# A layer kernel's first block: four more landing places for weight pieces, modulation work moved, the last output pieces and the norm done by 128 tokens

## What is computed

```python
mod = silu(c) @ w_ada + b_ada
sh_m, sc_m, gt_m, sh_f, sc_f, gt_f = split(mod, 6)
h = rms_norm(x, g_pre_mix) * (1 + sc_m) + sh_m
proj = h @ w_in                                # q, k, v of the two attentions "a" and "b"
mix = concat(fox_attention(...), moba_attention(...))
x = x + gt_m * rms_norm(mix @ w_out, g_post_mix)
h = rms_norm(x, g_pre_ffn) * (1 + sc_f) + sh_f
top_v, top_i = top_k(h @ w_router + b_router, 4)
y = sum over the 4 experts of gate * (swiglu(h @ w_gate_up[e] + b) @ w_down[e] + b)
x = x + gt_f * rms_norm(y, g_post_ffn)
# then two further blocks, which the change leaves as they are
```

## Time and profile before

| | |
|---|---|
| median of 3 runs | 2080.53 us (2080.02 to 2083.95) |
| the profiled execution, its own time | 2079.61 us |
| its span | 2077.8 us |
| busy: PE, DVE, ACT, POOL | 94%, 43%, 35%, 28% |
| first block up to the expert loop | 0 to 234 us |
| expert loop, 35 turns | 234 to about 1205 us |
| two further blocks | the rest |

### The profile page before, as it was taken

One profiled execution on the slowest core, in us unless ns is written; L12 is line 12 of the kernel. 1 busy time (PEld: TensorE's weight loads), 2 busy tenths in 40 slices (PEclk: granted clock), 3 DMA queues, 4 the chain that ended last, 5 costly groups with the idle time before them and its releaser, 6 DMA issues.

```text
span 2077.8 us, 28169 instructions
## 1 busy us (share of the span) xinstructions
PE 1951.1 (94%) x10657; PEld 1197.2 (58%) x10658; DVE 893.8 (43%) x1383; ACT 721.7 (35%) x1181; POOL 586.1 (28%) x622
## 2 busy tenths in 40 slices
PE   5997799999999999999998889999999999999998
PEld 2974333333333333333332259889888798898887
DVE  4644322111122222112211157557787566576983
ACT  2543211111111111111111055664665456556662
POOL 3230234433433434424434404000133021000440
PEclk7998799999999999999999989999999999999999
DMA  9978699999898999999999975446456553544553
GB/s 343 302 281 346 252 397 417 418 418 417 343 417 330 419 417 418 394 377 418 418 417 417 419 234 198 124 159 203 143 182 208 173 194 121 184 160 145 191 195 121
DMA packets 203045, 609.34 MB, mean 293 GB/s; under 512 B 10459, under 2 KB 115055, under 8 KB 166385
## 3 DMA queue, kind: packets, MB, share of 16 engines
q1 hardware_dynamic: 197360, 585.14, 73.8%
q0 software_dynamic: 5280, 22.19, 3.0%
q10 hardware_dynamic: 328, 0.95, 0.1%
HBM read 607.17 MB, written 9.26 MB: 297 GB/s over the span
## 4 chain that ended last, share of the span: by engine, by line
PE 71%; DMA 11%; SPq 6%; DVE 6%; ACT 4%; issue 2%; POOL 1%; ACTq 0%; DVEq 0%
PE bank L860 21%; PE bank L1192 15%; PE bank L897 10%; PE bank L1216 9%; DMA side<-in_w_gate_up 8%; PE bank L899 5%; SPq L699 4%; PE bank L1143 3%; SPq L706 2%; PE bank L1156 1%; DMA ring<-in_w_down 1%; DVE split L1662 1%; PE bank L1184 1%; PE bank L967 1%; ACT split L2101 1%
## 5 line engine op out<-in xcount | busy, mean ns | idle before, releaser
L1192 PE MATMUL bank<-ring,qkv 128*64 128x512 f32 x2240 | 504.2, 598 | 32.6 <-POOL ring L2384 32.5
L1192 PEld LDWEIGHTS bank<-ring,qkv 128*64 128x64 f32 x2240 | 152.5, 137 | 366.4 <-issue 268.8
L1662 DVE TENSOR_TENSOR split<-ring,split 128x2048 fp32r<-128x2048 f32 x104 | 249.9, 2403 | 115.5 <-ACT split L2101 115.5
L897 PE MATMUL bank<-hT_both,split 128*128 128x512 f32 x800 | 285.9, 401 | 6.7 <-DVE split L1662 6.7
L1216 PE MATMUL bank<-ring,qkv 128*64 128x512 f32 x1120 | 248.5, 595 | 1.3 <-DMA ring<-in_w_down 1.1
L2101 ACT ACTIVATE split<-ring 128x2048 fp32r<-128x2048 f32 x104 | 199.2, 1916 | 131.1 <-PE bank L860 126.1
L899 PE MATMUL bank<-hT_both,split 128*128 128x256 f32 x800 | 225.8, 282 | 0.0
L1636 DVE TENSOR_SCALAR qkv<-bank 128x512 f32<-128x512 f32 x35 | 24.2, 692 | 446.3 <-PE bank L1192 446.3
L2073 ACT ACTIVATE qkv<-qkv 128x512 f32<-128x512 f32 x35 | 22.1, 631 | 531.2 <-DVE qkv L1636 531.2
L1650 DVE SCALAR_TENSOR_TENSOR out_halves<-bank,small,out_halves 64x512 fp32r<-64x512 f32 x70 | 52.5, 750 | 330.2 <-ACT out_halves L2084 329.7
L897 PEld LDWEIGHTS bank<-hT_both,split 128*128 128x128 f32 x800 | 151.6, 190 | 45.1 <-DVE split L1662 8.0
(11 more groups left out here) (358 smaller groups left out, 3046.9 us busy)
## 6 DMA issues: line engine op xcount, KB each, us to landing
ring<-in_w_down SPq DMA_DIRECT2D x150, 1024.0 KB, 17.2
ring<-in_w_gate_up SPq DMA_DIRECT2D x70, 1024.0 KB, 19.8
probs<-in_w_gate_up SPq DMA_DIRECT2D x62, 1024.0 KB, 17.8
ring<-in_w_in SPq DMA_DIRECT2D x58, 1024.0 KB, 5.4
ring<-in_w_up SPq DMA_DIRECT2D x44, 1024.0 KB, 5.1
consts<-in_w_gate_up SPq DMA_DIRECT2D x31, 1024.0 KB, 20.5
side<-in_w_gate_up SPq DMA_DIRECT2D x31, 1024.0 KB, 22.4
qkv<-in_w_gate_up SPq DMA_DIRECT2D x31, 1024.0 KB, 21.7
```

Source lines behind the costliest of these rows:

```text
L897: pe.matmul(b[:, :].rearrange("p (h t) -> p h t", h=2), w_high[:, k, rows], hT_both[:, :, k, :], start=(k == 0), stop=False, skip_group_ch ...
L1192: last = pe.matmul(hidden[q][CAP * j:CAP * j + CAP, :], xgT[:, k % 4, k // 4, :], unit_at(k)[:, c:c + 512], start=False, stop=(k == KC - 1 ...
L1662: dve.tensor_tensor(low, unit_at(u % RING_L), high.bitcast(F32), ALU.subtract).then_inc(low_done, 1)
```

## The change

- Units get a home by table (`first_slots`). Units 26 to 29 go to places outside the ring: the `bands` constants, `qkv[:, 0:2048]`, `side`, `htok`. 25 to 29 can all be issued once the `w_in` product is through (27 after the scores of "a", 29 after the transposes of h). Units 30 to 33, 38, 39 take slots 2, 3, 4, 5, 0, 1; 34 to 37 take 2, 3 and the homes of 26 and 28. Each waits for the unit before it in its own slot.
- The last two `w_out` units become 38 and 39 in PE's count and 34 to 37 are the second half of modulation 2, but SP issues 38 and 39 ahead of 34.
- PE does modulation 1 and the first half of modulation 2 together, then `ada_rows(1)`, then the values of "b". Modulation 2's bank is held over that time.
- The last two `w_out` units are multiplied first for tile 0 only; then come the second half of modulation 2, unit 38 for tile 1, `ada_rows(2)`, unit 39 for tile 1.
- Norm, modulation and transposes go by tile. The modulated h is now x * gain, then * rstd + shift, so that the first pass needs no root. `turn_h` gives way to `turn_tile`; ACT copies g0 to g2, DVE g3.
- Expert units go out as slots come free: 4 and 5 of expert 0 after the second `w_out` unit, 2 and 3 two units later, staged 3 and 5 two after that; then 0, 1 and 8 to 11 after all 40; 6 and 7 after h and mod11.

```diff
+def first_slots():
+    at_bands, at_qkv, at_side, at_htok = range(RING, RING + 4)
+    order = [*range(FIRST_OUT_1 + 2), *OUT_1[2:], *range(FIRST_OUT_1 + 2, LAST_OUT_1)]
+    slots = {u: u % RING for u in range(26)}
+    slots.update({26: at_bands, 27: at_qkv, 28: at_side, 29: at_htok, 30: 2, 31: 3, 32: 4, 33: 5, 38: 0, 39: 1,
+                  34: 2, 35: 3, 36: at_bands, 37: at_side})
...
-            for u, source in enumerate(sources):
+            for u in first_order:
...
-                if u >= RING:
-                    sp.wait_ge(unit_done, u - RING + 1)
+                if first_held[u] is not None:
+                    sp.wait_ge(unit_done, first_held[u] + 1)
+                elif u == 26:
+                    sp.wait_ge(unit_done, KC + len(IN1))
+                elif u == 27:
+                    sp.wait_ge(*full("ascore17"))
+                elif u == 29:
+                    sp.wait_ge(*full("h3"))
...
             sp.wait_ge(*full("bturn7"))
-            for u in (0, 1, 3, 5):
+            for u in (0, 1):
                 load_staged(1, u)
             sp.wait_ge(*full("bout3"))
             load_staged(1, 4)
+            sp.wait_ge(unit_done, 33 + 1)
+            for u in (4, 5):
+                load_unit(0, u)
+            sp.wait_ge(unit_done, 35 + 1)
+            for u in (2, 3):
+                load_unit(0, u)
+            sp.wait_ge(unit_done, 37 + 1)
+            for u in (3, 5):
+                load_staged(1, u)
             sp.wait_ge(unit_done, first.units)
-            for u in range(RING):
+            for u in (0, 1, 8, 9, 10, 11):
                 load_unit(0, u)
             sp.wait_ge(h_ready, 3)
             sp.wait_ge(*emptied("mod11"))
-            for u in range(RING, MOE_UNITS):
+            for u in (6, 7):
                 load_unit(0, u)
...
-            ada(1)
+            ada_units(1, range(KC))
+            ada_units(2, range(KC // 2))
+            ada_rows(1)
             values("b", lambda h, c: proj1["vb"][:, c, h * DH:h * DH + DH])
-            ada_units(2, range(KC // 2))
...
+            for u in range(2):
+                mixed_in(u)
+                used(out_product(u, next_halves(2), range(4)))
+            last_halves = {}
+            for u in range(2, 4):
+                mixed_in(u)
+                last_halves[u] = unit_halves(2, OUT_1[u])
+                last = out_product(u, last_halves[u], (0, 1))
+            last.then_inc(tile_rows, 1)
             ada_units(2, range(KC // 2, KC))
+            used(out_product(2, last_halves[2], (2, 3)))
             ada_rows(2)
+            used(out_product(3, last_halves[3], (2, 3)))
             for tt in range(TT):
-                pe.wait_ge(h_ready, seen(h_ready))
-            turn_h([f"g{j}" for j in range(4)], htok)
+                turn_tile("g", tt)
...
-            post_norm([f"mix{j}" for j in range(4)], gate_m, x_mid)
+            def tile_modulated(tt):
+                dve.wait_ge(x_mid, seen(x_mid))
+                dve.tensor_tensor(htok[:, tt, :], x[:, tt, :], gain_f, ALU.mult)
+                tile_rstd(tt)
+                dve.scalar_tensor_tensor(out=htok[:, tt, :], in0=htok[:, tt, :], scalar=rstd[:, tt:tt + 1], in1=shift_f,
+                                         op0=ALU.mult, op1=ALU.add).then_inc(h_ready, 1)
+            layer_rows("mix", 0, gate_m)
+            layer_scaled("mix", 0, x_mid)
             ada(2, 2 * [gain(gain_f, gpre_f)])
             await_own("mod9")
-            await_x_mid()
-            row_scale()
-            modulated(gain_f, shift_f)
+            tile_modulated(0)
+            layer_rows("mix", 1, gate_m)
+            layer_scaled("mix", 1, x_mid)
+            tile_modulated(1)
+            await_full("g3")
+            leave(dve.tensor_copy(hT[:, 4:8, P:2 * P], bank("g3")[:, :].rearrange("p (k t) -> p k t", k=4)), "g3")
             ada_rows(2, 2, 2 * [gate(gate_f, gpost_f)])
...
-            square_banks([bank(f"mix{j}")[:, :] for j in range(4)], lambda: await_full("mix3"))
-            square_x(x_mid_ready)
-            for j in range(4):
-                copy(f"g{j}", hT[:, 2 * j:2 * j + 2, :])
+            act.activation(spare, eps, ACT.Sqrt)
+            layer_squares("mix", 0)
+            post_root(0)
+            pre_root(0, x_mid)
+            layer_squares("mix", 1)
+            post_root(1)
+            for g in range(2):
+                copy(f"g{g}", hT[:, 4 * g:4 * g + 4, 0:P])
+            pre_root(1, x_mid)
+            copy("g2", hT[:, 0:4, P:2 * P])
```

More of the change, by code:

```diff
@@ L147, in halves_slots @@
     return slots, owner
+def first_slots():
[4 more added lines that the diff above has]
+                  34: 2, 35: 3, 36: at_bands, 37: at_side})
+    turns, held_by, holds = {}, {}, {}
+    for u in order:
+        of_slot = holds.setdefault(slots[u], [])
+        held_by[u] = of_slot[-1] if of_slot else None
+        of_slot.append(u)
+        turns[u] = len(of_slot)
+    return order, slots, turns, held_by
 class Plan:
     def __init__(self):
-        self.tiles, self.units, self.jobs, self.uses, self.at = 0, 0, {}, [0] * 8, 0
+        self.tiles, self.units, self.jobs, self.uses, self.at, self.held = 0, 0, {}, [0] * 8, 0, None
     def bank(self, name):
+        if self.at % 8 == self.held:
+            self.at += 1
         b = self.at % 8
@@ L213, in ada_units @@
     def ada_units(r, n):
-        p.bank(f"ada{r}")
+        if f"ada{r}" not in p.jobs:
+            p.bank(f"ada{r}")
         for k in range(n):
@@ L240, in plan_first, with two_modulations @@
     p.attention("a", lambda: project(IN1[6:]))
[L241 to L242 removed]
+    def two_modulations():
+        ada_units(1, KC)
+        ada_units(2, KC // 2)
+        p.held = p.jobs["ada2"][0]
+        ada_rows(1)
+    p.attention("b", two_modulations)
     for j in range(4):
         p.bank(f"mix{j}")
[L245 removed]
+    for u in range(2):
         p.unit(*[f"mix{j}" for j in range(4)])
[L247 to L248 removed]
+    ada_units(2, KC // 2)
+    p.held = None
     ada_rows(2)
+    for u in range(2):
+        p.unit(*[f"mix{j}" for j in range(4)])
     for j in range(4):
@@ L1356, in row_scale @@
                 own(dve.reciprocal(rstd, root))
-            def post_norm(names, gate, signal):
-                mean_squares(names, gate, lambda last, j: leave(last, names[j]), bank)
-                row_scale()
-                await_own(names[-1])
-                for tt in range(TT):
-                    scaled(tt).then_inc(signal, 1)
-            def mean_squares(names, gate, done, bank_of):
-                for j, n in enumerate(names):
-                    tt, half = j // 2, slice(512 * (j % 2), 512 * (j % 2) + 512)
-                    dve.wait_ge(squares, seen(squares))
-                    if j == 3:
-                        pair = halves.rearrange("p (t a) -> p t a", t=TT)
-                        dve.tensor_tensor(meansq, pair[:, :, 0], pair[:, :, 1], ALU.add).then_inc(means, 1)
-                    done(dve.tensor_tensor(htok[:, tt, half], bank_of(n)[:, :], gate[:, half], ALU.mult), j)
             def scaled(tt, half=slice(0, D)):
@@ L1379, in scaled, with weighted, tile_rstd, layer_rows @@
                                                 in1=x[:, tt, half], op0=ALU.mult, op1=ALU.add)
-            def await_x_mid():
-                seen(x_mid)
-                dve.wait_ge(x_mid, seen(x_mid))
+            def weighted(tt, sources, gate, done):
+                for half in range(2):
+                    columns_ = slice(512 * half, 512 * half + 512)
+                    dve.wait_ge(squares, seen(squares))
+                    if half == 1:
+                        dve.tensor_tensor(meansq[:, tt:tt + 1], halves[:, 2 * tt:2 * tt + 1],
+                                          halves[:, 2 * tt + 1:2 * tt + 2], ALU.add).then_inc(means, 1)
+                    done(dve.tensor_tensor(htok[:, tt, columns_], sources[half], gate[:, columns_], ALU.mult), half)
+            def tile_rstd(tt):
+                dve.wait_ge(roots, seen(roots))
+                own(dve.reciprocal(rstd[:, tt:tt + 1], root[:, tt:tt + 1]))
+            def layer_rows(prefix, tt, gate):
+                if tt == 0:
+                    dve.wait_ge(tile_rows, seen(tile_rows))
+                else:
+                    await_full(f"{prefix}3")
+                names = [f"{prefix}{2 * tt + half}" for half in range(2)]
+                weighted(tt, [bank(n)[:, :] for n in names], gate, lambda last, half: leave(last, names[half]))
+            def layer_scaled(prefix, tt, signal):
+                tile_rstd(tt)
+                await_own(f"{prefix}{2 * tt + 1}")
+                scaled(tt).then_inc(signal, 1)
             dve.memset(eps, EPS)
@@ L1677, in hT_low @@
                     leave(last, n)
-            def weighted(tt, sources, gate, done):
-                for half in range(2):
-                    columns_ = slice(512 * half, 512 * half + 512)
-                    dve.wait_ge(squares, seen(squares))
-                    if half == 1:
```

(6 more changed lines are left out.)

134 lines of the change are left out of this document (56 added, 78 removed).

## The result

| | before | changed |
|---|---|---|
| median of 7 runs of each | 2080.02 us (2075.92 to 2083.95) | 2067.59 us (2065.86 to 2074.68) |
| the profiled execution | 2079.61 us | 2066.44 us |
| its span | 2077.8 us | 2064.6 us |

The ratio is 0.995, with a 95% interval of 0.9938 to 0.9963: the change takes 10.4 us off by the ratio, and 7.7 to 12.9 by the interval; the two medians are 12.4 us apart. The forecast was 2070.8 us, with a gain of 9.3. Of all runs on record one was slow, an execution of e4_loads_late (3535.55 us at a granted clock of 0.562); it is left out of that kernel's median and ratio.

What follows compares the result with a forecast made beforehand. Late `w_out` loads after DMA holes, then the norm tail, delay the expert loop, whose start moves everything. Router's result 9.3 us earlier, routing unchanged: 2079.61 - 9.3 = 2070.3, plus half the median's 0.9 offset: 2070.8; range 2067.5 to 2074.

Steps and rivals of the forecast that it cites:

- rival D: PE's clock stays up in the shorter gaps (2.5 us) and rises sooner in the first turn (1): 2067.3; chance 0.05.
- Loads up to the product: From 129.1 five units go out at once instead of one; product starts at 165.6, 5.1 us earlier.
- The product: 96 output matmuls 24.3 us, four modulation units 3.5, `ada_rows(2)` 1.1: end at 194.5, only 0.5 earlier.
- The tail: Norm, modulation and transposes after the product: last pass ends 201.2 for 209.34, router's result 205.2 for 214.46, 9.3 earlier.
- The tightest place: DVE modulates tile 0 to 195.1, just before tile 1's first square is there at 195.3; slack 0.2 us.
- The gate between g3 and the router's result: DVE's gate from mod10 and mod11, 1.28 us, formerly covered by transposes, now delays the router's result from 204.5 to 205.2.
- Routing: Router's result to first turn's bias: same instructions, unchanged at 19.9 us, so the bias starts at 225.1 for 234.34.
- The first turn: First turn of the expert loop: the moment PE's clock rises there can fall out 1.5 us either way.
- The cover: Expert loads land by 221.2, PE needs unit 0 at 227.1; if cover were gone, each microsecond late costs one.
- A: Order of work gains nothing up front, product still starts about 170.7; only norm by tile pays, 4.4: 2075.7; chance 0.11.
- B: Loads bind the loop's start, and PE's gain comes back as waits before L1192: about 2080; chance 0.07.
- C: Slower: PE reaches the expert loop at half clock, rising late; about 2090 if held through first turn; chance 0.04.

Runs made afterwards that it cites:

- e4_loads_late: Changed kernel, with all twelve ring loads of expert 0 and staged 3 and 5 issued only after all 40 units and h are ready; 2070.48 us, ratio 0.9947.
- e5: Kernel before, with POOL's subtraction for the low half of the experts' bias held back until PE has filled `places`; 2075.95 us, ratio 0.9984.
- e2: Changed kernel's tile order of product and norm, but old six slots, old modulation order and late expert loads; 2073.33 us, ratio 0.9974.
- e11: Changed kernel plus 8 needless matmuls ahead of the output product, to keep PE's clock up; 2067.78 us, ratio 0.9958.
- e10: Changed kernel, with all eighteen expert loads ahead of the loop issued as one block after the routing's `turned_gates`; 2085.57 us, ratio 1.0041.
- e1: The changed kernel once more, no edit; 2068.53 us, ratio 0.9955.
- e3: Kernel before plus the homes, moved modulation and expert loads as slots come free; product and norm as before; 2071.88 us, ratio 0.9969.

## Why the prediction was right

The mechanism and nearly every step held; the number was helped by luck. 2067.59 lies 3.2 us below the forecast, 0.1 inside the low end of the forecast's own range (2067.5 to 2074), and nearer to rival D's 2067.3, whose reason did not come about. And the start of the first turn, 225.1 forecast and 224.66 measured, is that near because two errors cancel: the router's result came 1.1 us late and the routing was 1.5 us shorter. Predicted and measured, in the changed kernel (whose trace is 0.46 us late already at the end of the `w_in` product, before anything that the change touches):

| step | predicted | measured |
|---|---|---|
| values of "b" start | 154.0 | 154.6 |
| product starts | 165.6 | 166.01 |
| product and what is in it end | 194.5 | 195.7 |
| last pass of the modulation ends | 201.2 | 202.43 |
| router's result taken | 205.2 | 206.28 |
| first turn's bias | 225.1 | 224.66 |
| whole time | 2070.8 | 2067.59 |

- **Loads up to the product.** Right: twelve units without a wait on DMA, and the product released by DVE's low copy.
- **The product.** 1.2 us late, 0.46 of it inherited. Its slow start stayed, as assumed; 72 matmuls took 19.17, where the prediction's terms give 18.9 (24.3 less 5.4), and each twelve of tile 1 took 2.95 for 2.7. `ada_rows(2)` did not wait: DVE's copy of the modulation row ended at 189.5, PE came at 191.70, slack 2.2 for a predicted 2.0.
- **The tail.** The tightest place was named with a slack of 0.2, and there was none: DVE's second pass over tile 0 ended at 196.49, and ACT had ended tile 1's first square at 196.35. It cost some 0.1 to 0.3. The 0.2 was a slip in the sum: from PE at `ada_rows(2)` (190.7) its own terms, 1.1 for the rows, 1.4 for the gains and two passes of 1.24, give 195.7 and not 195.1, which is after the square at 195.3. The gate between g3 and the router's result cost as said in kind, but only 0.2 of the 0.7 I had put there, since PE's router product ended at about 206.1 anyhow.
- **Routing.** "The same instructions", 19.9 us: this was the wrong step. The instructions were the same and took 18.4, for they stood otherwise to POOL's list. The prediction moved DVE's and PE's work past each other and did not lay POOL's three instructions beside it; e5 shows the cause, and it was worth 1.0 us in the changed kernel; the other 0.5 is clock.
- **The first turn.** Sized at no change, with 1.5 us either way. It was 2.8 us shorter, with the clock up before its first matmul. Over 14 profiles it is 28.53 to 28.55 in nine, all with the clock up before it. In four the clock rose only within the turn: 3.0 us into it in e2 (29.90), 5.8 in e4 (31.30), 6.0 in the kernel before (31.37) and 6.4 in e11 (31.58), so each microsecond at half clock cost a little under a half. The fourteenth, e10's 29.92, had the clock up and is longer by its two waits for loads. Neither the kernel nor the start decides when the clock rises: e4 and e1 differ by 2.8 us with the same program on PE. The band for this place was too narrow.
- **The cover.** Right in its result and too strict in its reason. I let it end where a unit is needed; e4 and e10 show that the reserve is the queue's idle time, about 21 us, and that what goes beyond it is paid in turns 2 to 6, which become DMA-bound, and not at the first turn's waits.
- **Rivals.** A (nothing won up front) is what e2 has, and its 0.9974 is 5.4 us for the 4.4 worked out; the changed kernel isn't there. B (the expert stream takes the gain) fell: the three more waits of the profiled run are absent in e1, and across all kernels but e10 the count wanders from 61 to 66 whatever the start. C (slower by the clock) fell; where the clock was at its worst, in e11, the first turn was 3.0 us longer than the changed kernel's, with the clock back at 229.4, 6.4 us into it. D was half there: the clock did not stay up at the product, but rose before the first turn.

The 10.4 us of the ratio agree with the 9.7 of the earlier start: 8.2 of them by the steps of the prediction, which had 9.3 there, and 1.5 in the routing, where it had none. What the profiled run has beyond that, the first turn's 2.8 and the 2.9 us behind the loop, is spread that other profiles show in either direction (the rest is 896.0 to 900.7 us in code that no experiment touches). How much of the difference the first turn's clock makes stays open: one profile per kernel can't say how often each length occurs. The mean granted clock of whole executions gives an estimate: it was 0.9789 over the 68 executions of the kernel before that were run beside the experiments and 0.9804 over 11 of the changed one (e1 included), and among the 68 a thousandth more of clock went with 1.3 us less of time. By that some 2 us of the difference go with the clock, in whatever stretch.

## What to carry to other kernels

Here a prefetch was worth as much as the loader's idle time ahead, not as the time until the consumer asks for the first piece. So count the idle time, and in a loop that turns between a bound by the engine and a bound by loads count the waits, each of which costs the difference of the two paces. When a step is moved, lay the lists of all engines beside it, POOL's too, since a vector instruction that starts beside a POOL one may have to sit that one out, in a stretch that nobody touched. Work put in to hold a clock has to end before the engine would be released anyway; else it eats what the clock gives.

## What the hardware showed that I had not expected

- DVE beside a POOL instruction: 0.42 to 1.46 us (two SBUF inputs), 0.17 to 0.58 in e5 and to 1.06 in e3 (a cast of 16 columns), 0.20 to 1.02 (tensor_scalar on 64 columns); an instruction with one of its inputs in a bank stayed at 0.20. In each case the DVE instruction ended 0.03 to 0.28 us after the POOL one, so a DVE instruction of 0.2 us can lose 0.8 or 0.9.
- An fp32 matmul of 256 columns against 128 x 128 weights took 0.43 us at full clock, in two records; the values' matmuls with 128 x 64 weights, two side by side (their records start 0.04 us apart), 0.23 each (L1035: 3.60 us for 16).
- The same program on PE comes to the expert loop at full clock in one profile and reaches it 5.8 us into the loop in another (e1 and e4, which differ only in when loads are issued): 2.8 us.
